# A 32-expert routed layer on one Trainium2 core: slots without a token get a row number behind a bound, and the experts' gathers and puts skip them

## What is computed

```python
def hier_moe(x, w_rg, w_re, w1, w3, w2):            # x: 512 tokens x 1024
    g_prob = softmax(xf @ w_rg)                     # 4 groups
    g_gate, g_idx = top_k(g_prob, 1)                # one group for a token
    e_logits = take the 8 logits of that group from xf @ w_re
    e_w, e_i = top_k(softmax(e_logits), TOP_K)      # TOP_K = 2 experts of the 8
    weights = g_gate * (e_w / sum(e_w))
    experts = g_idx * 8 + e_i
    ...
    # each expert: (silu(x @ w1[e]) * (x @ w3[e])) @ w2[e], times its weight, added to the token
```

## Time and profile before

| what | value |
|---|---|
| median of 3 runs (lowest to highest) | 1909.92 us (1909.56 to 1913.07) |
| the profiled execution: its time | 1908.89 us |
| its span in the trace | 1906.9 us |
| PE busy over the span | 1784.3 us (94%) |
| transfers: all, of them on POOL's queue | 333.44 MB, 17.04 MB |
| mean rate over the span | 175 GB/s |

### The profile page before, as it was taken

One profiled execution on the slowest core, in us unless ns is written; L12 is line 12 of the kernel. 1 busy time (PEld: TensorE's weight loads), 2 busy tenths in 40 slices (PEclk: granted clock), 3 DMA queues, 4 the chain that ended last, 5 costly groups with the idle time before them and its releaser, 6 DMA issues. The chain is left out here.

```text
span 1906.9 us, 23936 instructions
## 1 busy us (share of the span) xinstructions
PE 1784.3 (94%) x9580; PEld 994.8 (52%) x9580; DVE 755.3 (40%) x1471; ACT 545.7 (29%) x1114; POOL 150.1 (8%) x194
## 2 busy tenths in 40 slices
PE   8999878997978889999989999899999999899998
PEld 3333355464444444455565444577645544577763
DVE  2243377241421112143323325477524327365642
ACT  2111377222200011233213212455312232344420
POOL 1210000001111101111000014000000003000000
PEclk9999999988999999999999999999999999899999
DMA  7655858427999999999982222000200012000001
GB/s 267 220 191 176 127 128 79 158 110 311 420 420 418 418 417 418 420 420 421 398 336 72 88 88 88 1 2 1 103 0 34 22 61 68 21 1 1 1 23 44
DMA packets 92046, 333.44 MB, mean 175 GB/s; under 512 B 10208, under 2 KB 26720, under 8 KB 64928
## 3 DMA queue, kind: packets, MB, share of 16 engines
q1 hardware_dynamic: 78368, 304.27, 43.8%
q0 software_dynamic: 5200, 17.04, 2.3%
q10 hardware_dynamic: 8368, 10.60, 1.6%
HBM read 317.58 MB, written 14.30 MB: 174 GB/s over the span
## 5 line engine op out<-in xcount | busy, mean ns | idle before, releaser
L1042 PE MATMUL mix_ps<-arena 128*64 128x256 f32 x2048 | 237.9, 385 | 13.5 <-DMA arena<-in_w 5.8
L2089 PE MATMUL tail_ps<-arena 128*128 128x512 f32 x504 | 219.8, 592 | 0.7 <-DMA arena<-in_w_plg 0.7
L1042 PEld LDWEIGHTS mix_ps<-arena 128*64 128x64 f32 x2048 | 145.0, 138 | 99.9 <-issue 26.3
L930 PE MATMUL mix_ps<-arena,side 128*128 128x512 f32 x384 | 176.6, 613 | 1.4 <-DVE side L1381 1.4
L455 DVE TENSOR_REDUCE tail_small<-tail_ps 128x1 f32<-128x768 f32 x128 | 116.6, 952 | 119.6 <-PE tail_ps L336 119.6
L2089 PEld LDWEIGHTS tail_ps<-arena 128*128 128x128 f32 x504 | 94.9, 190 | 115.2 <-issue 114.7
L1054 PE MATMUL mix_ps<-arena 128*64 128x512 f32 x512 | 120.3, 613 | 27.7 <-DMA arena<-in_w 27.1
L930 PEld LDWEIGHTS mix_ps<-arena,side 128*128 128x128 f32 x384 | 72.6, 195 | 104.5 <-issue 86.3
L2089 PE MATMUL tail_ps<-arena,side 128*128 128x512 f32 (+2 forms) x320 | 119.6, 534 | 0.0
L540 ACT ACTIVATE arena<-tail_ps,tail_small 128x768 f32<-128x768 f32 x128 | 113.7, 898 | 5.9 <-DVE tail_small L455 5.9
L336 PE MATMUL tail_ps<-side,arena 96*128 96x512 f32 (+1 forms) x256 | 93.5, 510 | 6.3 <-ACT arena L540 5.7
(11 more groups left out here) (382 smaller groups left out, 2344.4 us busy)
## 6 DMA issues: line engine op xcount, KB each, us to landing
arena<-in_w SPq DMA_DIRECT2D x96, 2048.0 KB, 13.5
arena<-in_l_w_mod SPq DMA_DIRECT2D x16, 1024.0 KB, 5.1
arena<-in_l_w_in SPq DMA_DIRECT2D x16, 1024.0 KB, 7.0
arena<-in_w_in SPq DMA_DIRECT2D x12, 1024.0 KB, 9.3
arena<-in_l_w_mod SPq DMA_DIRECT2D x16, 512.0 KB, 4.5
residual<-bias_blocks SPq DMA_DIRECT2D x32, 224.0 KB, 12.3
arena<-in_l_w_in ACTq DMA_DIRECT2D x12, 512.0 KB, 11.0
arena<-in_l_w_out SPq DMA_DIRECT2D x6, 1024.0 KB, 5.1
```

The lines of the kernel that those rows point to most:

```text
L930: last = pe.matmul(ps[:, u % 4], oT[:, k, t * P:(t + 1) * P], weights.slot(W_IN[n, k // 4], 4, 512)[:, k % 4], start=(k == 0), stop=(k == ...
L1042: last = pe.matmul(out[h * CAP:(h + 1) * CAP, 0:H2], x, wb[:, k, h * H2:(h + 1) * H2], start=(k == 0), stop=(k == DK - 1))
L2089: last = pe.matmul(out, lhs(k), rhs(k), start=(k == 0), stop=(k == K - 1))
```

## The change

Both row numbers of an empty place now lie behind the end. `read_row` is 2048 lower, and the constant that is added to the list is 2048 + half in place of half, so that a place with a token gets the same number as before and one without gets 2048 or 2049. `index[:, 1]` is as before: an empty place has 2048 or more. Each of the 65 indirect transfers gets a bound (1023 for reading, 2047 for writing) and `oob_is_err=False`, by which a row number above the bound is to be left out and not taken for an error. The number of instructions and their order stay the same on every engine, but for one register write on POOL ahead of each indirect transfer, which hands it the bound.

```diff
-        read_row=f(2 * token),
+        read_row=f(2 * token - 4 * SEQ),
...
-            chain(dve.tensor_tensor(slot_rows, ps[:, 4, 0:N_EXPERTS], m["half"].to_broadcast([P, N_EXPERTS]), ALU.add))
+            chain(dve.tensor_tensor(slot_rows, ps[:, 4, 0:N_EXPERTS], m["spare_row"].to_broadcast([P, N_EXPERTS]), ALU.add))
...
-                chain(dve.tensor_tensor(over[:, 0:OVER], told_row(0), m["half"].to_broadcast([P, OVER]), ALU.add))
+                chain(dve.tensor_tensor(over[:, 0:OVER], told_row(0), m["spare_row"].to_broadcast([P, OVER]), ALU.add))
...
+            rows_read = dict(bounds_check=2 * SEQ - 1, oob_is_err=False)
+            rows_written = dict(bounds_check=4 * SEQ - 1, oob_is_err=False)
+
             def gather(e):
                 pool.indirect_dma_start(out=xg[:, e % 2], out_offset=None, in_=x_rows,
-                                        in_offset=bass.IndirectOffsetOnAxis(ap=index[:, 0, e:e + 1], axis=0)).then_inc(s["got"][e % 2], 16)
+                                        in_offset=bass.IndirectOffsetOnAxis(ap=index[:, 0, e:e + 1], axis=0), **rows_read).then_inc(s["got"][e % 2], 16)
...
                 pool.indirect_dma_start(out=y_rows, out_offset=bass.IndirectOffsetOnAxis(ap=index[:, 1, e:e + 1], axis=0),
-                                        in_=yb[:, e % 2], in_offset=None).then_inc(s["put"][e % 2], 16)
+                                        in_=yb[:, e % 2], in_offset=None, **rows_written).then_inc(s["put"][e % 2], 16)
...
-                                                in_offset=bass.IndirectOffsetOnAxis(ap=index[:, 0, STATIC:STATIC + 1], axis=0)).then_inc(d["got"], 16)
+                                                in_offset=bass.IndirectOffsetOnAxis(ap=index[:, 0, STATIC:STATIC + 1], axis=0), **rows_read).then_inc(d["got"], 16)
...
-                                        in_offset=bass.IndirectOffsetOnAxis(ap=current[:, 0:1], axis=0)).then_inc(d["got"], 16)
+                                        in_offset=bass.IndirectOffsetOnAxis(ap=current[:, 0:1], axis=0), **rows_read).then_inc(d["got"], 16)
...
-                                        in_=yb[:, STATIC % 2], in_offset=None).then_inc(d["put"], 16)
+                                        in_=yb[:, STATIC % 2], in_offset=None, **rows_written).then_inc(d["put"], 16)
```

## The result

| | before | after |
|---|---|---|
| median (lowest to highest), 4 runs each | 1909.74 us (1909.16 to 1913.07) | 1890.51 us (1887.29 to 1892.75) |
| ratio, 95% interval | | 0.9894 (0.9876 to 0.9913) |
| profiled execution: time, span, granted clock | 1908.89, 1906.9 us, 0.981 | 1889.70, 1887.9 us, 0.984 |

That is 19.2 us faster, where 10.5 were forecast and 1895.0 was the lower end of the range. Two later measurements of the same two kernels, with more runs, give 0.9927 (0.9906 to 0.9948) and 0.9931 (0.9908 to 0.9954), or about 14 us; they belong to the explanation.

The account below looks back on a forecast made before the run. Transfers were taken to set the pace from about 520 to 800 us, PE after that. -10.0 - 0.3 - 0.3 + 0.1 = -10.5, from 1909.92 to 1899.4 us; range for 8 in 10: 1895 to 1911.

Parts of the forecast that it names:

- What bounds the kernel: Expert loop: transfers set the pace from about 520 to 800 us, PE behind it; DMA share below 1 after 800 us.
- What is left out: POOL's queue: 17.04 MB and 5200 packets fall to 8.39 MB and some 3100 packets.
- Rival 1: Indirect transfers: descriptors for empty places are still made and engines spend the same packets; 1910.0 us, chance 0.19.
- The main term, 10.0: Puts 0 to 19 and gathers 3 to 23: rows left out save 10.0 us, between 13.8 and 0.
- rival 3: Expert loop: all 13.8 us count, and empty places' reads of one half row cost more; middle 1895, chance 0.10.
- the right sharing: Partitions over 16 engines: four neighbours and the four 32 higher to an engine, 14.5 full transfers saved, 9.4 us.
- The first gather and the end: PE's waits for the first gather (-0.3, ends 0 and -0.7) and the last w2 (-0.3, ends 0 and -1.3).
- What is added: POOL: a register write ahead of each of 65 transfers, plus the bound's cost; +0.1, ends 0 and +1.0.
- Rivals 2 and 4: 2: busiest engines keep their rows, about 1909.6, chance 0.12. 4: slow row-by-row check in POOL's descriptor making, 1915, chance 0.07.
- from the sum to the median: Last step: sum of -10.5 us taken from the runs' median, 1909.92, giving 1899.4 us.

Follow-up runs that it names:

- e8: The kernel before, with the bound handed only to puts of experts 21 and on; 367.65 us from put 0 to put 22 (before: 367.22).
- e2: The change without the gathers' bound, so only puts leave rows out; median 1900.31 us, 0.9976 of the kernel before.
- e3: The change without the puts' bound, so only gathers leave rows out; median 1898.87 us, 0.9969 of the kernel before.
- e10: The kernel with the change, but with each expert's filled places spread over the engines; median 1893.30 us, 0.9938 of the kernel before.
- e4: The kernel with the change, measured again beside the kernel before; median 1890.12 us, 0.9927 of the kernel before.
- e9: The kernel before, no bound, each empty place reading a half row of its own; 367.13 us from put 0 to put 22 (before: 367.22).
- e13: The kernel with the change once more, run beside the one with places spread; median 1892.28 us, 0.9931 of the kernel before.
- e1: Bounds on all 65 indirect transfers, but row numbers as in the kernel before, so all rows move; median 1904.71 us, ratio 1.0009.

## Why the forecast was wrong

**What bounds the kernel: right.** Transfers set the pace to about put 20, PE behind it. The engines' share stayed at 1.02 up to 785 us. It fell, to 0.83, only behind 900 us and not from 800 on; and it did not fall by some per cent before that, as was forecast for an uneven load. That the last third gives little fits e8 (at most 0.7 us in all) and the 1.1 us of the marks.

**What is left out: right in bytes, wrong in packets.** 8.41 MB were left (8.39 forecast), but the number of packets did not fall to 3100. Two left-out neighbours make a small packet of their own: 2088 more under 512 B. Rival 1's first half, that the descriptors are still made, is so true, at next to no cost: a full transfer left out saves 0.61 us, and 0.65 was the whole price that the forecast took.

**The main term, 10.0: under-sized.** It measured 11.3 to 11.5. The forecast had rival 3's 13.8 for an even load and 9.4 for the right sharing, and took a value next to the second. With 0.61 us a transfer the two rules give, for puts, gathers and both:

| | busiest engine | all bytes | measured |
|---|---|---|---|
| puts (e2) | 4.0 | 6.1 | 4.2 |
| gathers (e3) | 4.9 | 6.8 | 6.8 |
| both | 8.8 | 12.9 | 11.3, 11.4 and 11.5 |
| both, places spread (e10) | 11.5 | 12.9 | 12.1 |

So the sharing fits, but by it the rule that the busiest engine alone counts gives 8.8 where some 11.4 were measured: the value lies between the rules. Puts follow the first and gathers the second. Why they differ is open; no run tells it. Engines do run ahead of each other by some us, as the spread of 7.5 us shows. One explanation was not tested: the engines are not alike to begin with. In the kernel before, where every row is moved, a matrix' 16 completions are already 4.1 us apart at the end of the stretch. If the engine that is last there is not the one that keeps the most rows, the gain is more than the busiest engine saves. No view names the engine of a completion.

**The first gather and the end: right in sign, their sizes not settled.** The wait for the first gather fell from 8.83 to 8.32 us (0.3 forecast, 0.5 measured; 8.19 in e4), but kernels whose gathers move every row had 8.42 (e8) to 8.83 (e9). The wait for the last w2 fell from 1.31 to 0.66 us (0.3 and 0.65), but it was 1.09 in e4 and 0.80 in e13, and 0.66 to 1.07 in e8, e9 and e1. **What is added:** POOL's call grew from 0.99 to 1.02 us, hidden; e1 bounds all of it, with 1.0009 (0.9993 to 1.0025). **Rivals 2 and 4** are out: the stretch lost 11.5 us, and neither POOL's call nor the wait of 8.83 us grew by what rival 4 needs.

**The step that failed most is the last one, from the sum to the median.** "1909.92 - 10.5" takes the median of three runs for the kernel's time, and the range (1895 to 1911) holds only the unknowns of the transfers. But the kernel before takes anything from 1898.6 to 1915.0 us, by its granted clock, and 1905.1 in the median of 29. The range had no term for it, so that 1.3 us for each 0.001 of clock could carry the result out of it: 1890.5 with 1895.0 as the end. "A measurement of this kernel tells 0.2% (3.8 us) from no change" was also too narrow: with 4 runs each the two medians gave 19.2 us, with 6 and 29 runs 15.0. Of the 8.9 us between the forecast's 1899.4 and the measured 1890.5, 4.8 are this starting value: counted from 1905.1, the forecast's own sum would have given 1894.6. The other 4.1 are 1.4 in the main term, up to 0.6 at the ends, and a rest that is within what the clock moves. The change's own worth, 11 to 12 us, is near the forecast's 10.5; 5 to 8 of the 19.2 us in the result come with the clock and are not its doing, as far as the runs show.

## What to carry to other kernels

Where the DMA engines have no idle time, price a byte by the engine that carries it: leaving out rows pays if every engine loses some, and half of the bytes on half of the engines can be worth nothing. A queue's share of the whole span (2.3% here) says little; count its transfers inside the stretch where something waits for the engines. And before a forecast of under 1% is given a range, ask how the granted clock moves the time from run to run: marks inside the stretch that changed (here two puts, good to 0.7 us) settle in one execution what medians of whole runs need dozens for.

## What was not expected of the hardware

- A row behind the bound is not dropped from the queue. 5200 packets stayed 5200, and 2088 of them became small; the bytes halved. The small ones cost next to nothing (10 ns each): the queue's share fell from 2.3% to 1.2% of the span while its bytes fell to 49%.
- The same 32 matmuls (128x36) took 3.66 or 6.88 us by the clock granted, with PE busy without a break ahead of them in both executions.
- Engines get 7.5 us apart on one weight matrix in the mean with the real token counts (3.9 with the places spread), and the stretch was only 0.7 us shorter with the places spread.
